# A fused retention and latent-attention layer on one core: the input is left unnormalised and its per-token factor is applied further on

## What is computed

```python
xn = rms_norm(x, norm_mix_w)                       # x * rsqrt(mean(x^2)+eps) * gain
rq, rk, rv, rg, cq, ckv, kpe, ga, gb = split_columns(xn @ w_in)
rq = rope(rq, pos); rk = rope(rk, pos) * RET_DK ** -0.5
q = rms_norm(cq, q_norm_w) @ w_uq                  # 8 heads, 128 + 64 rotary
q = concat([q[..., :NOPE_DIM], rope(q[..., NOPE_DIM:], pos)])
ckv = rms_norm(ckv, kv_norm_w); kpe = rope(kpe, pos)     # both are outputs too
ret_y, mla_y, new_state = mixer_core(rq, rk, rv, q, ckv, kpe, w_ukv)
ret_branch = (head_group_norm(ret_y, ret_gn_w) * silu(rg)) @ w_ret_o
merged = sigmoid(ga) * ret_branch + sigmoid(gb) * (mla_y @ w_mla_o)
h = x + merged @ w_out
h = h + SwiGLU(rms_norm(h, norm_ffn_w)); y = rms_norm(h, norm_final_w)
```

## Time and profile before

| | |
|---|---|
| median of 3 runs | 2126.86 us (2126.3 to 2127.85) |
| the profiled execution | 2130.35 us |
| its span in the profile | 2128.5 us |
| TensorE busy | 2040.2 us (96%), 13370 matmul records |
| VectorE busy | 1076.0 us (51%) |
| ScalarE busy | 667.3 us (31%) |
| GpSimd busy | 331.4 us (16%) |
| DMA | 201.66 MB |

### The profile page before, as it was taken

One profiled execution on the slowest core, in us unless ns is written; L12 is line 12 of the kernel. 1 busy time (PEld: TensorE's weight loads), 2 busy tenths in 40 slices (PEclk: granted clock), 3 DMA queues, 4 the chain that ended last, 5 costly groups with the idle time before them and its releaser, 6 DMA issues. The chain is left out here.

```text
span 2128.5 us, 33254 instructions
## 1 busy us (share of the span) xinstructions
PE 2040.2 (96%) x13370; PEld 1965.3 (92%) x13370; DVE 1076.0 (51%) x1823; ACT 667.3 (31%) x1194; POOL 331.4 (16%) x302
## 2 busy tenths in 40 slices
PE   7879999998999989999999999989999999999997
PEld 7768788887999989999999999989999999999997
DVE  7966777765445433311112225675555565532247
ACT  5424444442222223311111123444444344310010
POOL 0110000001122210000000000344444444200000
PEclk9989999998999999999999999999999999999999
DMA  4511111116112113211151114323232323573422
GB/s 176 199 46 42 43 47 36 43 47 224 46 49 66 43 50 92 84 49 47 42 208 49 39 39 135 113 84 120 93 113 93 113 95 110 214 256 129 170 60 85
DMA packets 88846, 201.66 MB, mean 95 GB/s; under 512 B 11664, under 2 KB 42320, under 8 KB 85904
## 3 DMA queue, kind: packets, MB, share of 16 engines
q1 hardware_dynamic: 88720, 199.89, 27.6%
HBM read 141.71 MB, written 58.15 MB: 94 GB/s over the span
## 5 line engine op out<-in xcount | busy, mean ns | idle before, releaser
L837 PE MATMUL ps<-xn_hi,w_hi 128*128 128x384 f32 (+1 forms) x960 | 318.8, 332 | 6.7 <-DMA xn_lo<-xn_spill 4.1
L837 PE MATMUL ps<-sx_hi,t_hi 128*128 128x272 f32 x1056 | 305.7, 289 | 12.1 <-ACT u L1541 5.9
L839 PE MATMUL ps<-xn_lo,w_hi 128*128 128x384 f32 (+1 forms) x960 | 315.8, 329 | 0.0
L838 PE MATMUL ps<-xn_hi,w_lo 128*128 128x384 f32 (+1 forms) x960 | 315.5, 329 | 0.0
L838 PE MATMUL ps<-sx_hi,t_lo 128*128 128x272 f32 x1056 | 305.5, 289 | 0.0
L839 PE MATMUL ps<-sx_lo,t_hi 128*128 128x272 f32 x1056 | 304.4, 288 | 0.0
L837 PEld LDWEIGHTS ps<-sx_hi,t_hi 128*128 128x128 f32 x1056 | 200.2, 190 | 13.1 <-issue 6.9
L838 PEld LDWEIGHTS ps<-sx_hi,t_lo 128*128 128x128 f32 x1056 | 200.0, 189 | 0.1
L839 PEld LDWEIGHTS ps<-sx_lo,t_hi 128*128 128x128 f32 x1056 | 200.0, 189 | 0.0
L837 PEld LDWEIGHTS ps<-xn_hi,w_hi 128*128 128x128 f32 x960 | 181.9, 189 | 12.1 <-issue 5.7
L838 PEld LDWEIGHTS ps<-xn_hi,w_lo 128*128 128x128 f32 x960 | 182.2, 190 | 0.0
(11 more groups left out here) (251 smaller groups left out, 4727.9 us busy)
## 6 DMA issues: line engine op xcount, KB each, us to landing
w_stage<-in_weights SPq DMA_DIRECT2D x83, 512.0 KB, 3.8
y_spill<-hg_r SPq DMA_DIRECT2D x44, 544.0 KB, 3.4
yd<-y_spill SPq DMA_DIRECT2D x22, 1088.0 KB, 5.6
raw<-in_weights SPq DMA_DIRECT2D x22, 512.0 KB, 5.3
hg<-in_weights SPq DMA_DIRECT2D x22, 512.0 KB, 5.2
d_stage<-in_weights SPq DMA_DIRECT2D x24, 384.0 KB, 3.2
ym_spill<-out_hl SPq DMA_DIRECT2D x32, 256.0 KB, 2.4
xt<-in_x SPq DMA_DIRECT2D x8, 544.0 KB, 8.2
```

Of the source, the lines that this page charges most:

```text
L837: nc.tensor.matmul(out, wh, xh, start=start, stop=False, skip_group_check=onto)
L838: nc.tensor.matmul(out, wl, xh, start=False, stop=False, skip_group_check=onto)
L839: return nc.tensor.matmul(out, wh, xl, start=False, stop=stop, skip_group_check=onto)
```

## The change

x is never normalised. `xa_hi` and `xa_lo` (x times gain) are themselves written to HBM and read back later, and the token's factor r(x) = rsqrt(mean(x^2)+eps) is applied where the reference's result needs it. There are two forms of it: `x_col`, tokens on partitions, 9 columns of 128; and `x_inv`, tokens along the free axis, the same on all partitions.

- The sums over features become columns: `token_sums` makes 9 matmuls whose stationary operand is 128 tokens of the sum of squares and whose moving operand is one column of ones. The root and reciprocal become one power of -0.5 on GpSimd (`power`) over a 128x9 tile.
- `x_inv` is made from `x_col`: VectorE writes 9 diagonal blocks (`diag`), TensorE multiplies ones with them, ScalarE copies. The same is done for ckv (`kv_inv`). The norm of cq has no such rows.
- ckv is scaled once, by the factor of its own norm, with eps times r(x)^-2 in place of eps, so that x's factor cancels. cq is never scaled: `cqn_hi` and `cqn_lo` are split straight from PSUM, and the queries' factor goes into the exponential's scale and into the factor of the maximum, as a column for each tile of 128 queries.
- In retention, k's and v's factors and q's go into columns that were there before (`dcol`) or into the copy of v and the product with the mask.
- In stages E, F and G VectorE first multiplies the gate's PSUM with `x_inv`, and ScalarE's SiLU or sigmoid reads the product from SBUF. `x_inv` is written to HBM in stage A and read back at the start of retention.
- The items of stage A come in the order cq0, cq1, ckv0, ckv1, key, cq2, cq3. Head 0's projections come as keys, rotary, queries; its values moved into the attention's order. The first 12 units of projection use five PSUM banks in turn instead of two.

Cut to its core:

```diff
+A_ORDER = (0, 1, 4, 5, 6, 2, 3)
-    steps = [("S", 0, 8), ("S", 0, 0), ("P", 0, 8)] if head == 0 else []
+        steps = [("F", "M", 0, "V", 0), ("S", 0, 8), ("S", 0, 0), ("P", 0, 8),
+                 ("F", "M", 0, "V", 1), ("F", "M", 0, "V", 2)]
...
+            return (6, 7, 3, 4, 5)[u % 5] if u < 12 else 6 + u % 2
...
 @block.sync
-                sp.wait_ge(xs_low, t + 1)
-                sp.dma_start(xn_spill[:, 0, t, :], xs_hi[t % 2][:, :].bitcast(F32)).then_inc(xs_out[t % 2], 16)
-                sp.dma_start(xn_spill[:, 1, t, :], xt_lo[:, t, :].bitcast(F32)).then_inc(spill_out, 16)
+                wait_low(sp, t)
+                sp.dma_start(xn_spill[:, 0, t, :], xa_hi[:, t, :].bitcast(F32)).then_inc(spill_out, 16)
+                sp.dma_start(xn_spill[:, 1, t, :], xa_lo[:, t, :].bitcast(F32)).then_inc(spill_out, 16)
+                if t == 5:
+                    sp.wait_ge(root_done, NG)
+                    sp.dma_start(x_inv_spill, x_inv[:, :]).then_inc(x_inv_out, 16)
...
+            for b in range(2):
+                sp.wait_ge(o_out[b], 16 * 20)
+            sp.dma_start(x_inv[:, :], x_inv_spill).then_inc(x_inv_in, 16)
 @block.tensor
-            def feature_sums(k, src, chunks=GROUPS):
+            def token_sums(bank, src):
+                for a in range(TILES):
+                    L = P if a < TILES - 1 else DEC
+                    last = nc.tensor.matmul(ps[0:L, bank, a:a + 1], src[:, a * P:a * P + L], ones[:, 0:1],
+                                            start=True, stop=True)
+                last.then_inc(stat_done, 1)
+            def rows(first, groups):
...
+                    nc.tensor.matmul(ps[:, 7 - g % 2, 0:c1 - c0], ones[:, :], diag[:, c0:c1],
...
-            for kind in "KQRV":
+            for kind in "KRQ":
+                if kind == "R":
+                    pe.wait_ge(g_free, F_GATE)
+                    pe.wait_ge(summed, SUM_OUT)
+                    token_sums(2, q_sum)
 @block.scalar
+                    if j in CQ_AT:
+                        nc.scalar.activation(cqn_hi[:, t, c0:c1], src, ACT.Copy,
+                                             scale=gains[:, G_Q + t:G_Q + t + 1])
+                    nc.scalar.activation(dst[:, c0:c1], src, ACT.Square).then_inc(c_high, 1)
...
-                                             bias=negmax[0:nq, n % 2, 0:1], scale=SCALE,
+                                             bias=negmax[0:nq, n % 2, 0:1], scale=q_col[0:nq, tile:tile + 1],
...
-                        nc.scalar.activation(tmp[3][:, 0:c1 - c0], ps[:, k, 0:c1 - c0],
+                        nc.scalar.activation(g_silu[:, 0:c1 - c0], g_in[:, 0:c1 - c0],
                                              ACT.Silu).then_inc(g_act, 1)
 @block.vector
+            def rows(first, col):
+                for g in range(NG):
+                    for a in range(3 * g, 3 * g + 3):
+                        ins = nc.vector.tensor_scalar(diag[:, a * P:(a + 1) * P], eye[:, :], col[:, a:a + 1], None, ALU.mult)
+                    ins.then_inc(inv_done, 1)
...
-                                                -SCALE, None, ALU.mult).then_inc(max_done, 1)
+                                                nq_col[0:nq, tile:tile + 1], None, ALU.mult).then_inc(max_done, 1)
...
+            dve.wait_ge(p_free, ATT_END)
+            for h in range(RH):
+                nc.vector.tensor_scalar(z_col[:, h, :], x_col[:, :], dcol[:, h, 0:1], None, ALU.mult)
+                nc.vector.tensor_scalar(kd_col[:, h, 0:8], x_col[:, 0:8], dcol[:, h, 1:2], None, ALU.mult)
+                ins = nc.vector.tensor_scalar(kd_col[:, h, 8:9], x_col[:, 8:9], dcol[:, h, 2:3], None, ALU.mult)
...
+                        nc.vector.tensor_tensor(g_in[:, 0:w], ps[:, k, 0:w], x_inv[:, c0:c1], ALU.mult)\
+                          .then_inc(g_scaled, 1)
...
+            def gate_scaled_rows(i, u0, next_item):
+                for g, (c0, c1) in enumerate(GROUPS):
+                    dve.wait_ge(g_done, 6 * i + (u0 + g + 1))
+                    nc.vector.tensor_tensor(tmp[g][:, 0:c1 - c0], ps[:, g, 0:c1 - c0], x_inv[:, c0:c1], ALU.mult)\
+                      .then_inc(g_scaled, 1)
 @block.gpsimd
-            lows(KT, lambda t: cqn_lo[:, t, :], lambda t: cq_raw[:, t, :], lambda t: cqn_hi[:, t, :], 4)
+            def power(k, dst):
+                pool.wait_ge(var_done, k)
+                nc.gpsimd.tensor_tensor(dst[:, :], v_col[:, :], half_col[:, :], ALU.pow).then_inc(col_done, 1)
```

More of the change, by code:

```diff
@@ L181, in build @@
         dcol = at("dcol", CON + 3712, [RH, 3])
+        columns = at("columns", CON + 3776, [7, TILES])
+        x_col, v_col, eps_col, c_col, q_col, nq_col, half_col = [columns[:, k, :] for k in range(7)]
         G_MIX, G_Q, G_KV, G_GN, G_F, G_FIN = 0, 8, 12, 14, 22, 30
@@ L444, in build @@
         p_order = {}
[L445 to L446 removed]
+        for g in range(NG * 3):
+            p_order["M", 0, "KRQ"[g // NG], g % NG] = len(p_order)
         for h in range(MH):
@@ L710, in _ @@
                     item_in_loop(i, I_M1 + 2 + j)
-            for b in range(2):
-                sp.wait_ge(o_out[b], 16 * 20)
             for t in range(KT):
@@ L845, in block_product, with item_units @@
                                hi[:, k, c0:c1], lo[:, k, c0:c1], k == 0, k == blocks - 1)
-            def item_units(slot, n, bank, free, hi, lo, blocks=8, rows=P, between=None, between_at=0):
+            def item_units(slot, n, bank, free, hi, lo, blocks=8, rows=P, between=lambda g: None):
                 pe.wait_ge(w_low, n + 1)
@@ L856, in item_units @@
                     last.then_inc(g_done, 1)
-                    if between is not None and g == between_at:
-                        between()
+                    between(g)
             def streamed_item(slot, n, bank, free, hi, lo, ready=None, read=None):
@@ L1264, in _, with rows @@
+            def rows(first, dst, groups):
+                for g in groups:
+                    c0, c1 = GROUPS[g]
+                    act.wait_ge(stat_done, first // 3 * 4 + 1 + g + 1)
+                    nc.scalar.activation(dst[:, c0:c1], ps[:, 7 - g % 2, 0:c1 - c0], ACT.Copy).then_inc(root_done, 1)
             item(0)
@@ new lines, in variance, with rotate_key @@
+            def variance(k, bank, width):
+                dve.wait_ge(stat_done, 4 * k + 1)
+                nc.vector.scalar_tensor_tensor(v_col[:, :], ps[:, bank, 0:TILES], 1.0 / width, eps_col[:, :],
+                                               ALU.mult, ALU.add).then_inc(var_done, 1)
+            def rotate_key(g):
+                c0, c1 = GROUPS[g]
+                dve.wait_ge(g_done, 3 * KPE_AT + g + 1)
+                rotate(g, 3 * (KPE_AT % 2) + g, ROPE, ROPE // 2, cos64, sin64, c0, c1, g_free)
@@ new lines, in _ @@
+            x_sums(range(1, 4))
+            item(2)
+            x_sums(range(4, KT))
+            latent(0)
+            latent(1)
+            latent_sum(q_sum, 1)
+            item(3)
+            latent(2, (0, 1))
+            dve.wait_ge(stat_done, 1)
+            nc.vector.tensor_scalar(v_col[:, :], ps[:, 6, 0:TILES], 1.0 / D_MODEL, EPS, ALU.mult, ALU.add)\
+              .then_inc(var_done, 1)
+            dve.wait_ge(var_done, 1)
+            nc.vector.tensor_scalar(eps_col[:, :], v_col[:, :], EPS, None, ALU.mult).then_inc(set_up, 1)
@@ new lines, in _ @@
+            latent(2, (2,))
+            item(4)
+            dve.wait_ge(consts_in, 48)
+            dve.wait_ge(col_done, 1)
+            rows(0, x_col)
+            latent(3)
+            latent_sum(kv_sum, 3)
+            item(5)
+            dve.wait_ge(tables_in, 32)
+            rotate_key(0)
+            rotate_key(1)
+            dve.wait_ge(set_up, 2)
+            variance(1, 6, KV_LORA)
+            rotate_key(2)
+            item(6)
+            dve.wait_ge(col_done, 2)
+            rows(3, c_col)
@@ L1815, in shared_key @@
+            latent(5)
+            latent_sum(q_sum, 5)
+            dve.wait_ge(root_done, 6)
+            for t in range(2):
+                nc.vector.tensor_tensor(ckn[:, t, 0:TOK], ckv_raw[:, t, :], kv_inv[:, :], ALU.mult).then_inc(scaled, 1)
+            item(7)
             def shared_key():
@@ L2261, in _ @@
         def _(pool):
-            def lows(first, dst, src, high, tiles):
-                for t in range(0, tiles, 2):
-                    pool.wait_ge(norm_high, first + t + 1)
-                    nc.gpsimd.tensor_tensor(dst(t), src(t), high(t).bitcast(F32), ALU.subtract)\
-                      .then_inc(norm_low[0], 1)
             def add_products(r, dst, rows, width, freed, count):
```

509 lines of the change are left out of this document (251 added, 258 removed).

## The result

The changed kernel takes 2109.91 us (median of 4 runs, 2109.2 to 2110.89) against 2126.64 for the kernel before in the same session: ratio 0.9919, 95% interval 0.9905 to 0.9933. It is faster by 17 us. The profiled execution took 2109.2 us, its span is 2107.4.

What follows compares the result with a forecast made beforehand. TensorE, busy 96% of the span, bounds it, with time to win only in the first 161 us. Head -24.3, clock +2, attention +1, retention +1 make -20.3 us: 2110.0 profiled, 2106.5 against the median; range 2098 to 2119.

Steps and rivals of the forecast that it cites:

- the first rival: Before the first scores: rotary chain slower and clock sinks in the pause, gain only 10 us, 2117; chance 15%.
- Stage A and the keys: Projection stage: TensorE's own work end to end, nobody late, reaches head 0's keys at 104.2 us.
- The one pause: Before head 0's first scores: TensorE waits 4.8 us for the rotary part, until 130.3 us.
- The first transpose: Start of attention's transposes: comes at 137.1 us instead of 161.4, 24.3 us less, before 2 us added for clock.
- Attention: 72 exponentials with a column scale, 86 ns longer each: 0 to 6.2 us on the path, taken as 1.
- The factor of the maximum: nothing: Attention: the factor of the maximum is the same instruction with another operand, so costs nothing.
- Retention 1 us, gates 0: Retention: small column products and reading x_inv back cost 0 to 2 us, taken as 1; gate products hidden, cost nothing.
- the rival of the gate chain: Stages E, F, G: added product makes items longer than TensorE's 11.8 us, kernel slower, 2140 at 13.2 us; chance 5%.
- From the profiled execution to the median: Whole kernel: 2110.0 us for the profiled execution, less 3.5 us to the median, gives 2106.5 us.
- The clock in the one-column sums: Stage A and head 0: each of three sets lowers the clock, gain 4 to 7 us smaller, 2111 to 2114; chance 12%.
- The heavier rotary chain: Before the first scores: 1 us more per rotary group, 4 from clock, 3 in attention's first tiles; 2117; chance 15%.
- nothing is won: Ahead of attention: a late wait, likely weights or ckv scaling, replaces the old ones; 2123 to 2130; chance 6%.

Runs made afterwards that it cites:

- experiments 9 to 11: Changed kernel with head 0's queries between rotary parts (2107.41 us); with second values unit before the first scores (2106.06); with queries' sums behind first rotary unit (2107.55).
- experiments 3 and 4: Changed kernel with exponent's scale and subtrahend's factor both numbers again (2103.35 us); with only the exponent's scale a number, subtrahend keeping its column (2105.24 us).
- experiment 4: Changed kernel with only the exponent's scale a number again, the subtrahend keeping its column: 2105.24 us.
- experiment 8: Changed kernel with the gates' product by x's factor made a second time on VectorE (all 24 in output gate, 32 of 48 in merging stages): 2110.44 us.

## Why the prediction was right, and where its sizes were off

Forecast 2106.5 in 2098 to 2119, measured 2109.9: faster, in the range, 3.4 us off. The profile is as foretold: the waits on the serial chains ahead of attention are gone, and one pause is left. How much each chain was worth is not shown. The upper end of the range is not what its terms give: the first rival is 2117, and sets of 3.5 us, 6 us of clock and half of the exponentials come to 2115.

*Stage A and the keys.* Said 104.2, came at 103.8, with no wait over 0.5 us between the first item and the keys. A set of sums was taken at 2.6 us (1.3 to 3.5) and measured 2.05: at 142 ns a load I was too high, and the 1.9 us by the Trainium skill, TensorE: Matmul & The Clock Gate, section LDWEIGHTS (loading the stationary operand), was nearer; the measured 0.114 us a load is 7% over its figure. The rows of `x_inv` took 1.45 + 0.70 us, as said. GpSimd's power of nine columns is 1.81 us, inside 0.6 to 5.1, and hidden.

*The one pause.* Said 4.8 us until 130.3; measured 6.4 until 130.56. The end was right, the start was not: TensorE, whose sets and keys are shorter than I took them, got there earlier. I had the queries' low parts ahead of the last rotary pair; experiments 9 to 11 show that this order, the idle engine and the sums ahead of the chain were 0.9, 2.4 and 2.1 us, there for the taking.

*The first transpose.* Said 137.1, then 2 us for the clock beside it; it came at 137.3 with the clock loss in it (two blocks of values in 4.37 us, where I had 3.5). The term's size was right, and the shorter sums paid for it.

*Attention.* This term was mis-sized: 1 us, measured 2.7 between the profiles (0 to 6.2 was the bound). I argued that with TensorE idle for 20 of 335 us few exponents can be on the path. Of the 10.4 us that the columns add (6.6 on ScalarE, 3.8 on VectorE) 3.2 were, by experiments 3 and 4. TensorE's idle time is largely at the places where the chain from the maximum over the exponent to the transposes ends last (14.5 of 23 us), so it grows with it. That only 2.7 us show is in part luck of the clock, which gave 2.5 us back.

*The factor of the maximum: nothing.* That was wrong. The instruction is 60 ns longer, and by experiment 4 this is about 1.9 us of attention at equal clock.

*Retention 1 us, gates 0.* 0.7 and -0.2 by the means; experiment 8 shows the gates' room, and the rival of the gate chain did not come, by a wide margin.

*FFN: no term.* The sum has none, since the change does nothing there; 1.7 us were lost in it and at the end, by the clock.

*From the profiled execution to the median.* The sum gave 2110.0 for a profiled execution, and it took 2109.2. That agreement is partly luck: the execution of the kernel before that the sum starts from was a long one, its span 5.4 us over that of the second profile. By the means of the pairs the spans differ by 18.1 us and not 20.3: the head gave 0.8 more than the 22.3 that I had with the clock, attention took 1.7 more than said, the FFN and the end 1.7. Then I took off the 3.5 us by which before's profiled execution lay over its median. Up to 2.2 of these lay in the head, whose first transpose came that much later than in the second profile; the change removes that stretch, so they were already in my 24.3 us. The medians differ by 16.7 us, and the last 1.4 are scatter of single executions as far as is known.

*The rivals.* The clock in the one-column sums is real, but occasional: 4 of 30 sets. As a case (every set, 4 to 7 us) it did not come; when the sets are twice as long every one is followed by it, 1.4 us each. The heavier rotary chain and "nothing is won" did not come.

## What to carry to other kernels

Where TensorE waits at several places of a serial prologue, write down its own work end to end and add only the waits that the new order leaves: that gave the keys, the scores and the first transpose within 2 us. Then look at the pause that is left, for in it there is room for work that stands just behind it, and a shorter pause also gives the clock back. A number that becomes a column costs time on each instruction that reads it, on VectorE as on ScalarE; in a chain that ends in TensorE's waits expect a share of it in the total (3.2 of 10.4 us here). Take out the time at the lower clock level before two stages are compared, and don't carry the scatter of one execution over to the other kernel.

## What the runs showed that was not expected

- A column in place of a number made 72 exponents 91 ns longer (717 to 808 ns) and 64 products of one column on VectorE 60 ns longer (154 to 214 ns).
- Nine one-column float32 matmuls leave 18 records at 0.114 us each with the clock at 1.00, but sets of 36 records were followed by 4 us at a mean clock of 0.57 to 0.62, in 3 of 3 places, with TensorE busy throughout.
- Behind one and the same wait of 5.9 us in the FFN the mean clock of the next 6 us was 0.75 or 0.76 in four profiles and 0.50 to 0.52 in nine, 1.5 us of time.
- Less time at the lower clock level hid half of attention's loss: 5 us at equal clock, 2.7 measured.
